# Hymba layer kernel on one core: attention values computed transposed, extra constant matmuls in the routing's waits, the last expert's tile written as its own code

## The reference

```
hn = rms_norm(x, norm_mix_g); proj = hn @ w_in
att = sliding-window attention with sinks   # 8 heads of 64, 2 kv heads, window 128
h_m = chunked mLSTM                         # 4 heads, keys 64, values 128, normed, times sigmoid(o_m)
x = x + concat([att, h_m]) @ w_out
x = x + hier_moe(rms_norm(x, norm_ffn_g))   # 4 groups x 4 experts, top 2 experts of one group
```

## Time and profile before

| | |
|---|---|
| median of 3 runs (range) | 923.83 us (923.13 to 925.13) |
| the profiled execution's time | 923.86 us |
| its span | 922.1 us |
| granted TensorE clock, mean | 0.973 of 2.4 GHz |
| busy: PE, DVE, ACT, POOL | 866.4, 616.2, 563.5, 249.7 us |

### The profile page before, as it was taken

How to read it: one execution, slowest core, us unless ns; L and a number is a source line. 1 busy time by engine, 2 the same in 40 slices (tenths; PEclk the granted TensorE clock), 3 DMA queues, 4 the chain that set the end, 5 groups by cost and what they waited for, 6 DMA issues and landing times.

```text
span 922.1 us, 18021 instructions
## 1 busy us (share of the span) xinstructions
PE 866.4 (94%) x5330; PEld 696.3 (76%) x5331; DVE 616.2 (67%) x1258; ACT 563.5 (61%) x1004; POOL 249.7 (27%) x395
## 2 busy tenths in 40 slices
PE   5899999999999998999973999999999999999994
PEld 4788888898989887788852776776777787677873
DVE  3766666666667667543578866773769599775992
ACT  3664655646373757221241866793889799787991
POOL 5102011010102010000032244543344544455442
PEclk9999999999999998999985899999999999999998
DMA  9800010101010152354473887786598999879973
GB/s 329 257 24 24 25 46 0 45 0 45 0 45 23 47 183 69 138 172 136 149 284 111 321 283 231 249 294 174 218 352 314 324 392 391 272 282 337 393 260 69
DMA packets 54526, 168.41 MB, mean 183 GB/s; under 512 B 9440, under 2 KB 11808, under 8 KB 54496
## 3 DMA queue, kind: packets, MB, share of 16 engines
q1 hardware_dynamic: 47264, 143.13, 41.8%
q0 software_dynamic: 7232, 24.92, 10.4%
HBM read 143.49 MB, written 24.54 MB: 182 GB/s over the span
## 4 chain that ended last, share of the span: by engine, by line
PE 89%; DVE 5%; issue 2%; DMA 2%; ACT 1%; POOL 0%; POOLq 0%; SPq 0%; ACTq 0%; DVEq 0%
PE bank_j L1059 15%; PE bank_j L1061 14%; PE bank_j L1060 14%; PE bank_j L1471 7%; PE bank_j L1121 6%; PE bank_t L1053 4%; PE bank_j L1127 4%; PE bank_s L1487 3%; PE bank_o L1199 3%; PE bank_t L1192 2%; PE bank_s L1059 2%; PE bank_s L1061 2%; PE bank_s L1060 1%; PE bank_o L1061 1%; PE bank_o L1060 1%
## 5 line engine op out<-in xcount | busy, mean ns | idle before, releaser
L1059 PE MATMUL bank_j<-w_high,rows_high 128*128 128x512 f32 x512 | 208.3, 407 | 4.9 <-DVE w_low L1680 2.6
L1061 PE MATMUL bank_j<-w_high,rows_low 128*128 128x512 f32 x512 | 202.6, 396 | 0.0
L1060 PE MATMUL bank_j<-w_low,rows_high 128*128 128x512 f32 x512 | 202.6, 396 | 0.0
L600 POOL TENSOR_TENSOR tick<-mhalf 1x1 f32<-1x1 f32 x176 | 87.8, 504 | 201.8 <-DVE lg L2124 71.8
L1059 PEld LDWEIGHTS bank_j<-w_high,rows_high 128*128 128x128 f32 x512 | 97.7, 191 | 36.3 <-issue 12.1
L2012 DVE TENSOR_TENSOR w_low<-w_res,w_high 128x1024 fp32r<-128x1024 f32 x96 | 114.2, 1219 | 7.0 <-ACT w_high L701 7.0
L1061 PEld LDWEIGHTS bank_j<-w_high,rows_low 128*128 128x128 f32 x512 | 97.8, 191 | 21.3
L1060 PEld LDWEIGHTS bank_j<-w_low,rows_high 128*128 128x128 f32 x512 | 97.7, 191 | 18.7 <-issue 0.2
L701 ACT ACTIVATE w_high<-w_res 128x1024 fp32r<-128x1024 f32 x96 | 97.5, 1050 | 0.8 <-PE bank_j L1061 0.8
L1121 PE MATMUL bank_j<-hnT,w_res 128*128 128x128 f32 x512 | 60.3, 276 | 0.0
L1121 PEld LDWEIGHTS bank_j<-hnT,w_res 128*128 128x128 f32 x512 | 58.4, 192 | 0.9
(11 more groups left out here) (380 smaller groups left out, 1833.5 us busy)
## 6 DMA issues: line engine op xcount, KB each, us to landing
w_res<-in_w_gate_dram SPq DMA_DIRECT2D x48, 512.0 KB, 7.8
w_res<-in_w_up_dram SPq DMA_DIRECT2D x48, 512.0 KB, 7.9
bias<-in_w_down_dram SPq DMA_DIRECT2D x32, 512.0 KB
slot_b<-in_w_gate_dram SPq DMA_DIRECT2D x16, 512.0 KB
PT<-in_w_up_dram SPq DMA_DIRECT2D x16, 512.0 KB
gmix<-in_w_down_dram SPq DMA_DIRECT2D x16, 512.0 KB
h<-in_w_down_dram SPq DMA_DIRECT2D x16, 512.0 KB
hn<-in_x_dram SPq DMA_DIRECT2D x8, 512.0 KB, 3.3
```

The lines of the kernel that those rows point to most:

```text
L600: pool.tensor_tensor(tick[:, len(ticks):len(ticks) + 1], mhalf[0:1, 0:1], mhalf[0:1, 0:1], ALU.mult)
L1059: pe.matmul(out_, ah, bh, start=start, stop=False)
L1060: pe.matmul(out_, ah, bl, start=False, stop=False)
L1061: return pe.matmul(out_, al, bh, start=False, stop=stop)
```

## The change

1. **Values transposed.** `values` takes v (128 x 64) as the stationary operand and PT of two heads (256 columns) as the moving one, 4 matmuls a round, the two kv heads' outputs in the two partition halves of O0. O0 now holds head columns by queries. ACT copies it unscaled into the first half of `mix` (`head_copy`); DVE's `prob_scales`, put between the second PT copy and `state_weights`, makes the reciprocals and spreads them over 512 columns (`scales`, in lg); PE transposes these (`sums_T`, 4 transposes into T0, between `values(1)` and `state_values`); DVE multiplies `mix` by T0. PE's transposes of hn now wait for the previous tile's `attention`.
2. **The first half of `mix_rows` is thus already transposed**: `mix_T` makes 4 transposes instead of 8, `mix_high` and `mix_low` read the first half from hn. `load_mix` waits for DVE's `mix_low` of the tile before rather than for the transposes. The first four pieces of w_out are loaded in the order of the new rows, each by two DMAs of 64 rows.
3. **Constant products**: `keep_busy(n)`, n matmuls of two constants (128 x 128, float32) into S1 that nobody reads: 7 before tile 7's h2 transposes, 15 before `positions`, 13 before and 13 after `late_slots`, 4 after `tile_order`, 9 after the first `rows_T`.
4. **Last expert**: PE's loop runs over 15 experts, the last is written out. Its full tile makes no `rows_T`, no row split, no gather. `last_down` orders the down steps so that S1 is complete two steps before O0. POOL waits on constants, without ticks, for two other semaphores before the last scatter, and at the very end for the scatter alone.

```diff
-                def values(r, done):
-                    for j in range(G):
-                        h, g = round_head(r, j), j // RH
-                        for w, slot in ((0, v), (1, u)):
-                            ins = pe.matmul(O0[:, h * HD:(h + 1) * HD], PT[:, j, w, :],
-                                            vw[:, slot, g * HD:(g + 1) * HD], start=(w == 0), stop=(w == 1))
+                def values(r):
+                    for w, slot in ((0, v), (1, u)):
+                        for g in range(KVH):
+                            pe.matmul(O0[g * HD:(g + 1) * HD, r * RH * P:(r + 1) * RH * P], vw[:, slot, g * HD:(g + 1) * HD],
+                                      PT[:, g * RH:(g + 1) * RH, w, :], start=(w == 0), stop=(w == 1),
+                                      skip_group_check=True)
+                def sums_T():
+                    pe.wait_ge(dve_arc, t + 1)
+                    for c in range(G):
+                        ins = pe.transpose(T0[:, c * P:(c + 1) * P], scales[:, c * P:(c + 1) * P], ident[:, :])
+                    ins.then_inc(pe_o, 1)
...
-                    values(1, pe_o)
+                    values(1)
+                    sums_T()
                     state_values()
...
+            def head_copy(t):
+                act.wait_ge(pe_o, t + 1)
+                wait(act, st_mix, 16 * t)
+                cp(mix[:, 0:AW], O0[:, :]).then_inc(act_att, 1)
...
                     if into_last:
                         out_high(1)
                 if main:
+                    head_copy(t)
                     state_squares(t, t + 2)
...
+            def prob_scales(t):
+                dve.wait_ge(act_p1, t + 1)
+                wait(dve, pe_o, t)
+                chain(dve.tensor_tensor(arc[:, :], asum[:, :], aes[:, :], ALU.add))
+                chain(dve.reciprocal(arc[:, :], arc[:, :]))
+                dve.wait_ge(pe_pT1, t + 1)
+                dve.tensor_copy(scales.rearrange("p (c g d) -> p c g d", c=G, g=KVH),
+                                arc[:, :].rearrange("p (g c) -> p c g", g=KVH).unsqueeze(3)
+                                .to_broadcast([P, G, KVH, HD])).then_inc(dve_arc, 1)
             def attention(t):
                 dve.wait_ge(pe_o, t + 1)
+                dve.wait_ge(act_att, t + 1)
+                dve.tensor_tensor(mix[:, 0:AW], mix[:, 0:AW], T0[:, :], ALU.mult).then_inc(dve_att, 1)
...
                     pT_copy(t, pe_pT1, dve_pT1)
+                    prob_scales(t)
                     state_weights(t)
...
             def mix_T(t):
                 pe.wait_ge(ld_mix, 16 * (t + 1))
-                transposes(hn, pe_mixT)
+                for i in range(4):
+                    ins = pe.transpose(T1[:, i * P:(i + 1) * P], hn[:, AW + i * P:AW + (i + 1) * P], ident[:, :])
+                ins.then_inc(pe_mixT, 1)
...
             def load_out(i):
-                sp.dma_start(slot_out[i], w_out[0, i * P:(i + 1) * P, :]).then_inc(ld_piece[i], 16)
+                if i < G:
+                    for g in range(KVH):
+                        sp.dma_start(slot_out[i][g * HD:(g + 1) * HD, :], heads_out[g, i, :, :]).then_inc(ld_piece[i], 16)
...
+            def keep_busy(n):
+                for _ in range(n):
+                    pe.matmul(S1[:, 0:P], ident[:, :], tri[:, :], start=True, stop=True)
+            keep_busy(7)
             h2_T(TILES - 1)
             router(TILES - 1)
             router_sum(TILES - 1)
+            keep_busy(15)
             positions(TILES - EARLY, 2)
+            keep_busy(13)
             late_slots()
+            keep_busy(13)
...
             tile_order()
+            keep_busy(4)
...
             rows_T(0)
+            keep_busy(9)
...
+            def last_down(t):
+                pe.wait_ge(y_ready, 2 * t)
+                for n, (c, half) in enumerate(((0, 0), (0, 1), (1, 0), (1, 1), (2, 0), (3, 0), (2, 1), (3, 1))):
...
-            tile(end, NE - 1, halves, st_full, row_s, yb)
+            pwait(ld_g, 16 * end + 32)
+            pool.wait_ge(st_full, 16 * (NE - 1))
+            pwait(st_half, 16 * halves)
+            pick(row_s, end)
+            pwait(pool_rowg, 2 * end + 1)
+            pool.wait_ge(act_om, TILES + 1)
+            pool.wait_ge(dve_bias, 2)
+            scatter_add(row_s, yb, st_full)
             pool.wait_ge(st_full, 16 * NE)
-            pwait(st_half, 16 * halves)
-            pwait(ld_g, 16 * end + 48)
```

More of the change, by code:

```diff
@@ L363, in hymba_layer_program @@
         half_order = [0, 2, 1, 3]
+        LAST_E = NE - 1
+        landed = [64 if i < G else 48 if i < OUTP else 32 for i in range(PIECES)]
         def split_free(i):
@@ L723, in mix_high @@
                 act.wait_ge(pe_mixT, t + 1)
-                for b in range(2):
-                    cp(MX[u][0][:, 4 * b:4 * b + 4, :].rearrange("p a b -> p (a b)"), TB[b][:, :]).then_inc(act_mixT, 1)
+                for b, src in enumerate((hn[:, 0:AW], T1[:, :])):
+                    cp(MX[u][0][:, 4 * b:4 * b + 4, :].rearrange("p a b -> p (a b)"), src).then_inc(act_mixT, 1)
             def route_exp(count, n):
@@ L1044, in _ @@
                 tile(last, e, split)
[L1045 removed]
+            tile(half_tiles(LAST_E) + LAST_E, LAST_E, lambda a, b: None)
         @block.tensor
@@ L1161, in body @@
                     pe.wait_ge(dve_hn, t + 2)
+                    wait(pe, dve_att, t)
                     transposes(hn, pe_hnT)
@@ L1256, in body @@
                     pe.wait_ge(dve_att, t)
-                    values(0, pe_pv0)
+                    values(0)
                     first_out([4])
@@ L1506, in _ @@
             rows_T(0)
+            keep_busy(9)
             pe.wait_ge(dve_tab, 1)
-            with pe.Fori(0, NE) as e:
+            with pe.Fori(0, NE - 1) as e:
                 expert(e)
+            expert(LAST_E)
         @block.vector
```

73 lines of the change are left out of this document (49 added, 24 removed).

## The result

The changed kernel takes 916.37 us (median of 4 runs, 915.26 to 917.47), the kernel before 924.19 us beside it: ratio 0.9922, interval 0.9909 to 0.9935, 7.8 us less. The same kernel, run again beside the experiments, gave 0.9935 (0.9916 to 0.9955). The forecast was 912.7 in a range of 907 to 918: the sign, the range and the terms of the first stage held, but 3.4 of the forecast 11.2 us did not come (5.2 by the repeat's ratio). The profiled execution is the 917.47 one (span 915.6), 1.10 above the median.

What follows compares the result with a forecast made beforehand. PE's own work, busy 94% of the span, was taken to set the loop's pace. Gains of 5.1, 1.45, 2.7, 2.0 and 1.15 less 1.2 summed to 11.2 us off 923.86: 912.7, range 907 to 918.

Steps and rivals of the forecast that it cites:

- the bounds of the copy: Loop tiles: DVE's copy over 512 columns, taken as some 0.4 us, 0.69 at worst; 0.3 a tile in the range.
- rival B: w_out loads: three late pieces come at half their rate in 64-row transfers; 2.0 us more, 914.7; 17%.
- rival D: Clock drops in one to three places where PE waits longer, as tile 7's start; 1.7 us each, 914.4 to 918; 13%.
- the output tile of 13.25 us: Output stage: a sign to show the forecast, a tile of 13.25 us instead of 13.7.
- Loop: First stage, tiles 0 to 5: shorter values rounds, with DVE's weights limiting, save 0.85 us a tile, 5.1 in six.
- rival E: Values matmuls: the two halves don't overlap, so the 5.1 and 1.0 us gains fall away; 918.8; 5%.
- Tile 6: First stage: head copy behind out_high(1) makes a new chain, squares 1.2 us later; 1.2 us lost, bounds 0 and 3.
- Tile 7: First stage: shorter values rounds give 1.0 us, four fewer transposes in mix_T(1) 0.45; 1.45 us saved.
- Output stage: PE works there without waits, so removed transposes save 0.45 us in each of six tiles; 2.7 us.
- Routing: Constant products in PE's gaps keep full clock for transposes and positions; 2.0 us saved, ends -1 and 4.3.
- rival F: Routing: constant products start at low clock, take twice their time and delay the next product; 919; 4%.
- End: Last expert: eight transposes and two ticks go, the scatter's tick may be offset; 1.15 us saved, between 0.5 and 2.

Runs made afterwards that it cites:

- run 4: The changed kernel with the four transposes of the sums in each tile issued twice; 920.36 us, ratio 0.9971 to the kernel before.
- the control: The changed kernel, unchanged, run again on the same chip beside the experiments; 916.39 us, ratio 0.9935 to the kernel before.
- run 2: The changed kernel with ACT's copy of tile 6's attention values ahead of the conversion of w_out's piece 1; 915.88 us, ratio 0.9918 to the kernel before.
- run 7: The changed kernel with the router behind the output product's first block and ACT's copies and conversions reordered in tiles 6 and 7; 912.71 us, ratio 0.9884.
- run 5: The changed kernel with w_out's first four pieces each loaded by one 128-row transfer, rows in old order; 940.08 us, ratio 1.0186, whole time not comparable.
- run 3: The changed kernel with the router of tiles 0 to 5 issued after the first block of the second half's output product; 915.25 us, ratio 0.9909.
- run 6: The changed kernel with more constant products in the routing, to fill PE's waits; 916.14 us, ratio 0.9928 to the kernel before.
- run 11: The changed kernel with the router moved, ACT's new order in tiles 6 and 7 and more constant products, w_out in halves; 910.65 us, ratio 0.9864.
- run 8: The changed kernel with the last expert's full tile as in the kernel before; 917.72 us, ratio 0.9945.
- run 10: The changed kernel with router moved, ACT reordered, more constants, one 2-by-64-row load per w_out piece, and a POOL operation before the last scatter; 937.23 us, ratio 1.0144.

## Why the prediction was right, and where its sum was not

The range was met, but not for its reasons: it was drawn for the bounds of the copy, of tile 6 and of the routing and for rivals B and D, and the largest shortfall came in the output stage, for which it allowed nothing. That the time is inside is in part luck. Of the signs that the prediction named, the longer wait at tile 7's start (4.26 us) and the loop's gain near 0.85 came; the output tile of 13.25 us (13.70 measured) and a clock of 1.0 through the routing did not.

*Loop, 5.1 forecast, 4.6 measured.* Right in size, by the wrong bound, so the size is in part luck. I let DVE's weights end last; they are done 0.4 us early, and run 4 shows that PE's products pace the place. By PE's own products the forecast's numbers give 1.25 a tile (1.7 less 0.45); a round took 1.01 us and not 0.9, and the conv products ahead of each took 0.09 more, which brings it to 0.77. The four matmuls of a round do overlap in the two halves, as the half-tile rows said (0.25 us each, 0.23 there), and rival E is out.

*Tile 6, -1.2 forecast, -1.1 and -0.9 measured.* The mechanism is right: the new chain behind the conversion of piece 1, from its rows, 1.5 us longer than the old one and started 0.4 to 0.6 earlier. Against the control, run 2 gets 1.1 us back and run 7 2.6. Rival B's slower halves are in it with 0.7 us, not 2: I priced the spacing of pieces, but ACT has other work between them. The sum had put the halves at nothing, and with whole loads the loss would have been 0.2 (run 5, 44.04 for 43.84), so the close fit owes something to chance.

*Tile 7, 1.45 forecast, 1.1 measured.* The scores after the longer wait ran at half the clock (2.08 for 1.16), as rival D had it for this place. Whether that drop cost the 0.3 to 0.4 us that are missing stays open. By the windows 8.5 us of tile 7 pass at half the clock in after, in two drops, for 6.8 before, also in two; in the repeat it is 5.7 us in one drop, but a wait of 1.12 us for ACT is new. Run 7 takes the first drop away and brings waits of its own. In the nine traces with ACT in this order tile 7 takes 34.8 to 36.2 us, so single pairs can't settle 0.3.

*Output stage, 2.7 forecast, nothing measured (0.4 lost in this trace, 0.1 gained in the repeat's).* This is the step that failed. I had written that PE works there without waits, and so took every removed transpose as gain. There was no wait because the eight transposes were just as long as ACT's and DVE's copies beside them: 1.00 us from their start to the router's, 0.89 to the end of the later copy. I named no cover for this edit and did not ask what it covered. With the router moved, runs 3 and 7 bring 1.9 and 2.2 us of it, and the tile takes 13.26 us where the forecast had 13.25.

*Routing, 2.0 forecast, 0.2 in the first trace and 1.5 in the second.* The products of constants do what I said when the clock holds, and whether it holds depends on the execution: mean clock 0.88 in one, 0.96 in the other, for counts that leave PE idle for 1.5 to 2.2 us between groups. In the first, one group ran at half the clock and made the transposes 0.5 us late, rival F in one place and small; it is also one of the signs that the prediction had named for being wrong, a constant product that ends after the operand of its successor. My error was to give full clock to all of it: where it held throughout, the piece gained 1.8 and 1.9 us (runs 6 and 11).

*End, 1.15 forecast, 0.2 to 0.3 in the two pairs, 0.3 to 0.9 against run 8.* The 0.7 at PE came. The scatter starts 0.39 later behind the weighing instead of 0.3 sooner; "the direct wait may cost as much" had allowed for nothing gained, not for a loss. From there to the span's end it is 11.8 and 11.9 us with the old end and 11.4 to 11.9 with the short one, so the ticks' 0.35 is about 0.2.

So the sum of 11.2 shrinks mainly by 2.6 to 3.1 at the output stage, 0.5 to 1.8 in the routing and 0.9 at the end: to 4.8 and 6.3 by the pieces of the two traces, to 7.8 and 6.0 by the two ratios.

## What to carry to other kernels

Work that an engine does between its order to another engine and the answer is cover. Before counting its removal as gain, take the other engine's copy time from its row: if the two are equal, nothing is gained until the waiter is moved behind other work. When a new operation goes onto an in-order engine next to one that waits for a transfer, put it ahead of that wait, then look who is late next; here it was the same engine's conversions for a later stage. Moved into a gap of 3 us, they still raised a wait there from 0.83 to 2.26 us, so look at that place again too. A transfer's pattern should have its large dimension outermost; here two plain halves cost 0.7 us, the one transfer over 2 times 64 rows more than 20.

## What the runs showed that I had not expected

- The load over 2 times 64 rows moved some 50 GB/s, against 230 for two halves in flight and 380 for whole loads.
- Products of constants between waits do not hold the clock by being there: with gaps of 1.5 to 2.2 us it fell three times in one trace (to half for some 3.4 us each) and once in the other; with the counts of run 6 it stayed at 1.00 in all three traces (runs 6, 10 and 11).
- PE stood 0.45 to 1.55 us with no releaser where the unrolled last expert begins, in three of twelve traces with it, and POOL's small operation ahead of the last but one scatter took 4.51 us in after where it takes 1.10 (in the control another one took 4.50). Both are outside of what these runs can explain.
- In the written-out end the last scatter starts 1.56 to 1.61 us behind the weighing's start, in all twelve traces, with and without an operation between; in the general tile 1.17 and 1.18. Why, stays open.
